# Two stacked transformer-like blocks on one core: half of the transposed activations made on VectorE

## The reference

```
h = rmsnorm(x, g_ffn1);  x = x + 0.5 * (silu(h @ w1) * (h @ w3)) @ w2      # stage "ffn0", hidden width 2816
h = rmsnorm(x, g_mix);   x = x + mixer(h @ w_in) @ w_o                     # stage "mix"
h = rmsnorm(x, g_ffn2);  x = x + 0.5 * (silu(h @ w1) * (h @ w3)) @ w2      # stage "ffn1"
```

## Time and profile before

| | |
|---|---|
| time, median of 3 runs | 2257.19 us (2256.69 to 2257.74) |
| span of the profiled execution | 2255.2 us (its time outside the span is not recorded) |
| TensorE matmuls, busy | 2249.8 us, 100%, 11686 instructions |
| TensorE weight loads, busy | 1920.7 us, 85% |
| VectorE, busy | 1546.0 us, 69%, 2179 instructions |
| ScalarE, busy | 1238.9 us, 55%, 1489 instructions |
| DMA | 417.61 MB, mean 185 GB/s |
| TensorE clock granted | full speed in every slice |

### The profile page before, as it was taken

The page is one execution under the profiler, slowest core; times in us unless marked ns, Lnnn a source line. Parts: engine busy times, 40 slices in busy tenths (PEclk is TensorE's granted clock), DMA queues, the critical chain, the costliest instruction groups (busy, mean ns, idle before and its releaser), DMA issues.

```text
span 2255.2 us, 28960 instructions
## 1 busy us (share of the span) xinstructions
PE 2249.8 (100%) x11686; PEld 1920.7 (85%) x11686; DVE 1546.0 (69%) x2179; ACT 1238.9 (55%) x1489; POOL 0.2 (0%) x4
## 2 busy tenths in 40 slices
PE   9999999999999999999999999999999999999999
PEld 8888888888888888888888888888888888888887
DVE  7764567765774566775776599767657747976773
ACT  7644445554653544654554576465555537755652
POOL 0000000000000000000000000000000000000000
PEclk9999999999999999999999999999999999999999
DMA  7556455555555455554555553545555555345553
GB/s 264 205 198 219 168 191 175 196 196 174 191 187 205 168 175 199 187 197 169 201 190 202 192 169 129 206 155 191 206 177 187 185 180 195 109 172 196 184 191 126
DMA packets 176213, 417.61 MB, mean 185 GB/s; under 512 B 16816, under 2 KB 20784, under 8 KB 176080
## 3 DMA queue, kind: packets, MB, share of 16 engines
q1 hardware_dynamic: 175936, 415.76, 53.3%
q10 hardware_dynamic: 144, 0.00, 0.0%
HBM read 414.66 MB, written 1.05 MB: 184 GB/s over the span
## 4 chain that ended last, share of the span: by engine, by line
PE 98%; DMA 1%; DVE 0%; SPq 0%; ACT 0%; issue 0%; DVEq 0%
PE psum L666 25%; PE psum L602 17%; PE psum L604 17%; PE psum L603 17%; PE psum L667 13%; PE psum L677 3%; PE psum L634 2%; PE psum L685 2%; PE psum L976 1%; DMA xt_in<-t_xt_dram 0%; PE psum L797 0%; DMA raw<-t_gate_up_1a_dram 0%; PE psum L954 0%; PE psum L817 0%; PE psum L944 0%; PE psum L966 0%
## 5 line engine op out<-in xcount | busy, mean ns | idle before, releaser
L1646 DVE TENSOR_TENSOR split_w<-raw,split_w 128x2048 fp32r<-128x2048 f32 (+1 forms) x405 | 881.1, 2182 | 285.8 <-ACT split_w L1176 284.9
L1176 ACT ACTIVATE split_w<-raw 128x2048 fp32r<-128x2048 f32 (+1 forms) x405 | 736.2, 1828 | 311.1 <-PE psum L604 288.2
L666 PE MATMUL psum<-xt,split_w 128*128 128x512 f32 x2464 | 859.2, 393 | 0.1
L667 PE MATMUL psum<-xt,split_w 128*128 128x256 f32 x2464 | 689.2, 280 | 0.0
L666 PEld LDWEIGHTS psum<-xt,split_w 128*128 128x128 f32 x2464 | 461.2, 187 | 104.3 <-DVE split_w L1646 1.3
L667 PEld LDWEIGHTS psum<-xt,split_w 128*128 128x128 f32 x2464 | 465.3, 189 | 0.3
L602 PE MATMUL psum<-split_w,xt 128*128 128x512 f32 (+1 forms) x736 | 289.5, 393 | 0.0
L604 PE MATMUL psum<-split_w,xt 128*128 128x512 f32 (+1 forms) x736 | 283.7, 385 | 0.0
L603 PE MATMUL psum<-split_w,xt 128*128 128x512 f32 (+1 forms) x736 | 283.6, 385 | 0.0
L602 PE MATMUL psum<-split_w,ht_hi 128*128 128x512 f32 x700 | 272.9, 390 | 0.0
L604 PE MATMUL psum<-split_w,ht_lo 128*128 128x512 f32 x700 | 272.5, 389 | 0.0
(11 more groups left out here) (278 smaller groups left out, 1951.2 us busy)
## 6 DMA issues: line engine op xcount, KB each, us to landing
raw<-w_in_dram SPq DMA_DIRECT2D x180, 512.0 KB, 4.4
raw<-t_gate_up_1b_dram SPq DMA_DIRECT2D x88, 512.0 KB, 4.1
raw<-t_gate_up_2a_dram SPq DMA_DIRECT2D x88, 512.0 KB, 4.1
raw<-t_gate_up_2b_dram SPq DMA_DIRECT2D x88, 512.0 KB, 4.1
raw<-t_gate_up_1a_dram SPq DMA_DIRECT2D x84, 512.0 KB, 4.1
raw<-ffn_w_down_dram SPq DMA_DIRECT2D x80, 512.0 KB, 4.2
raw<-w_a_dram SPq DMA_DIRECT2D x40, 512.0 KB, 4.4
raw<-w_b_dram SPq DMA_DIRECT2D x40, 512.0 KB, 4.4
```

The costliest lines, as they stand in the source:

```text
L666: nc.tensor.matmul(bank, whi[:, slot, w], xt[:, c, :, :], start=c == 0, stop=False)
L667: last = nc.tensor.matmul(bank[:, 0:T], wlo[:, slot, w], xt_hi[:, c, :], start=False, stop=c == DC - 1)
L1176: nc.scalar.activation(whi[:, u % HL, 0:n], raw[:, r, 0:n], ACT.Copy).then_inc(hi_done, 1)
L1646: nc.vector.tensor_tensor(wlo[:, u % HL, 0:n], raw[:, r, 0:n], whi[:, u % HL, 0:n], ALU.subtract).then_inc(w_ready, 1)
```

## The change

Half 0 of `x` at a stage change is turned by VectorE, into a new SBUF tensor, and ScalarE and VectorE read that tensor in place of PSUM. VectorE's transpose turns blocks of 32x32 inside a group of 32 partitions; here its input lies in one partition quarter and its output in another, so 16 instructions (4 quarters of the tokens by 4 quarters of the features) turn the whole half. Each handles 32 partitions by 256 elements. Half 1 stays on TensorE.

```diff
@@ buffers, behind the other tensors of the ffn stage
+        xturned = sb(ffn, "xturned", [P, DC // 2, T])
@@ tensor: x_transposes(stage) keeps half 1 alone; the three calls for half 0 go
                 blocks(u, 0, 1, HT, (0, 1), True, False, False)
-                if next_stage != "end":
-                    eng.wait_ge(done, e.after(done, ("x", next_stage, 0)))
-                    x_transposes(next_stage, 0)
                 blocks(u, 2, 1, HT, (2, 3), False, False, True)
@@ tensor, mix1 and mix2
-                wide(u, 1, MERGED, 0, 2)
-                eng.wait_ge(done, e.after(done, ("x", "ffn1", 0)))
-                x_transposes("ffn1", 0)
-                wide(u, 1, MERGED, 2, 4)
+                wide(u, 1, MERGED)
@@ scalar: def x_hi(stage, half)
+                if half == 0:
+                    eng.wait_ge(done, e.after(done, ("turned", stage)))
+                    for c in range(4):
+                        last = nc.scalar.activation(xt_hi[:, c, :], xturned[:, c, :], ACT.Copy,
+                                                    scale=vecs[:, gain + c:gain + c + 1])
+                    last.then_inc(acted, e.mark(acted, ("xt", stage, 0)))
+                    return
@@ vector: def x_lo(stage, half)
+                if half == 0:
+                    eng.wait_ge(acted, e.after(acted, ("xt", stage, 0)))
+                    for c in range(4):
+                        last = nc.vector.scalar_tensor_tensor(
+                            out=xt_lo[:, c, :], in0=xturned[:, c, :], scalar=vecs[:, gain + c:gain + c + 1],
+                            in1=xt_hi[:, c, :].bitcast(F32), op0=ALU.mult, op1=ALU.subtract)
+                        if c % 2:
+                            last.then_inc(done, e.mark(done, ("xt", stage, 0, c // 2)))
+                    return
@@ vector: new function
+            def x_turned(stage):
+
+                eng.wait_ge(done, e.after(done, ("x", stage, 0)))
+                for q in range(4):
+                    for r in range(4):
+                        src = x[32 * q:32 * q + 32, :, 0:512].rearrange("p m (c f) -> p m c f", c=4)
+                        dst = xturned[32 * r:32 * r + 32, :, :].rearrange("p c (m t) -> p m c t", m=MT)
+                        last = nc.vector.transpose(dst[:, :, :, 32 * q:32 * q + 32], src[:, :, :, 32 * r:32 * r + 32])
+                last.then_inc(done, e.mark(done, ("turned", stage)))
@@ vector, ffn_vector at s = 27 (split of unit 30 comes right behind)
                             add_to_x(2, 0, hidden=True).then_inc(done, e.mark(done, ("x", next_stage, 0)))
+                            x_turned(next_stage)
@@ vector, mix1 and mix2
                 add_to_x(0, 0).then_inc(done, e.mark(done, ("x", "ffn1", 0)))
+                x_turned("ffn1")
                 x_lo("ffn1", 0)
                 split(u0 + 33)
```

More of the change, by code:

```diff
@@ L639, in chunk, with x_transposes @@
                 return lambda m: src[:, m, c * P:(c + 1) * P]
-            def x_transposes(stage, half):
+            def x_transposes(stage):
                 for j in range(2):
-                    c = 4 * half + 2 * j
+                    c = 4 + 2 * j
                     turn(psum[:, 6 + j, :], (chunk(x, c), chunk(x, c + 1))).then_inc(
-                        small, e.mark(small, ("xt", stage, half, j)))
+                        small, e.mark(small, ("xt", stage, 1, j)))
             def mix_first(u0):
@@ L652, in mix_first @@
                 eng.wait_ge(done, e.after(done, ("x", "mix", 1)))
-                x_transposes("mix", 1)
+                x_transposes("mix")
                 wide(u0, 0, XT, 1, 2)
@@ L729, in first_two @@
                         eng.wait_ge(done, e.after(done, ("x", stage, 1)))
-                    x_transposes(stage, 1)
+                    x_transposes(stage)
                     for b in range(2):
```

## The result

The changed kernel takes 2279.04 us (2277.28 to 2279.67, 4 runs) against 2257.28; the ratio is 1.0095 (1.0082 to 1.0108): **slower by 21.8 us**. The profiled execution has a span of 2277.1 us, 21.9 more than before. A second set of runs (experiment 8) gave 1.0096 (1.0081 to 1.0111).

What follows compares the result with a forecast made beforehand. TensorE was taken to bound the kernel (98% of the chain). Ffn ends -1.5, change of block +2.9 and mixers +12.3 gave +13.7 us on the 2255.2 span, 2268.9; with 2.0 for the median 2270.9 us, range 2257 to 2285.

Steps and rivals of the forecast that it cites:

- T: Total time of the 16 VectorE transposes at a stage change, forecast 7.3 us, without overlap and 0.03 between.
- What TensorE gains: TensorE loses 8 transposes at each of 11 changes: 9.7 us, the most the change can gain.
- a set: The 8 TensorE transposes of one half at one stage change, costed at 0.88 us.
- The second rival: VectorE transposes overlap at one element a cycle, T = 5.5: sum +1.0, 2258.2 us; no change, chance 0.13.
- Ends of ffn stages: Six plain ends: TensorE stalls 0.63 us for unit 30's split against 0.88 saved, -0.25 each, -1.5 for six.
- Ends of mixers: Four ends: TensorE waits for unit 33's split, idle 4 us in each; +3.1 each, +12.3 for four.
- The change of block: From block 1 to 2, once: the split of unit 31 comes late and TensorE waits; net +2.9 us.
- The fourth rival: Clock falls to 1.2 GHz behind each 4 us stall: sum +35, 2293 us; chance 0.09 shared with longer transposes.

Runs made afterwards that it cites:

- experiment 8: The changed kernel, unaltered, run again beside the kernel before: 2278.56 us, ratio 1.0096.
- experiment 5: Kernel before, with VectorE turning half 0 only at the seven ffn ends, splits put ahead of the transposes and x_hi: 2250.52 us, ratio 0.9971.
- experiment 4: Changed kernel with each transpose writing the quarter it reads, so xturned is arranged wrongly: 2262.05 us, ratio 1.0019.
- experiment 3: Changed kernel plus 15 matmuls that nothing reads on TensorE at each of the four mixer ends: 2268.2 us, ratio 1.0048.
- experiments 1 to 9: All the follow-up runs, on edits of the changed kernel or the kernel before; their traces' wait at the start was 0.3 to 2.2 us.

## Why the prediction came out as it did

The sign, the places and the waits were right and the time lay in the range; the size was not: +13.7 forecast, +21.8 measured. That it lay in the range is in part luck. The range reached up to 2285 for transposes longer than forecast, T up to 8.5; T was 7.2, and what took the time to 2279 was the clock, which the range left to a rival.

- **What TensorE gains.** 88 transposes go, and a set is worth 0.88 us: experiment 5 shows -0.88 seven times.
- **T.** Forecast 7.3, measured 7.2, from 0.436 and not 0.425 a piece and a spacing of 0.45. That they would not overlap, read from two gaps in the earlier trace rows, decided whether there is a loss worth speaking of: experiment 4 has T = 5.7 and is 3.9 us slower than before, not 21.8. The second rival, overlapped transposes and no change, was refuted for this kernel and nearly met by experiment 4.
- **Ends of ffn stages.** -0.25 forecast, -0.46 measured: T 0.1 shorter and a restart 0.1 quicker than my sum.
- **Ends of mixers.** +3.1 forecast, +2.9 measured with the clock full (experiment 3). The chain was read rightly: `x_hi`, ScalarE's split, VectorE's split. From `x_hi`'s start to VectorE's split it took 3.54 us (362.19 to 365.73) and not 3.41, since ScalarE's reads of `xturned` were slower, 1.71 for 1.57, where I had priced the reads from SBUF at nothing.
- **The change of block.** +2.9 forecast; by waits 0.4 + 3.0 - 0.88 = +2.5, and the rest of the measured 3.9, 1.4, I put down to the clock; no filler was tried here.
- **The step that was mis-sized: the clock.** The fourth rival had it at +22 over the forecast and shared 0.09 of the chance. It happened at all five of the forecast's stalls that came to 2.8 us and more. Its size was 6.9 us at the mixers and 1.4 at the change of block, 8.3 in all, since a fall cost 1.4 to 2.3 us and not a unit's doubled time, 5.4. It belonged into the forecast's own sum: a stall of 4 us in an engine that had never stalled was the forecast's main term, and I priced its length only.
- **The start**, +2.8 in the profiled run, 1.1 of it again the clock, was in no step; the traces of experiments 1 to 9 speak for chance.

The forecast's terms as measured: -2.7 + 2.5 + 11.5 = +11.3; with 8.3 for the clock 19.6; the start and the small steps, 2.8 - 0.5, are the rest.

## What to carry to other kernels

An engine with 30% of idle time can take over work and still stop the bound one: look at what is queued behind the new work and when it is wanted, and put that first. The same 16 transposes were worth +4.1 or -0.88 us at the change of block by their order alone. When a change makes TensorE wait, ask for the wait's length and for the clock behind it, and measure the two apart with filler matmuls.

## What the runs showed of the hardware

Stalls of TensorE and the granted clock behind them: at 3.7 us the clock fell to half in all twelve cases of three traces; at 2.8 in all five; at 2.2 to 2.4 in three of six (two of the four in experiment 4, and at the start in the changed kernel's trace but not in experiment 3's); at 1.8 or less in none. Full clock came back some 3 to 6 us after TensorE went on. The fall can also come behind the stall: in the last mixer of the changed kernel TensorE went on at 2088.55 us and was granted 1.00 from 2088.5 to 2090.0, then 0.52 from 2090.0 to 2093.5. The Trainium skill (TensorE: Matmul & The Clock Gate, "HAM oscillation") describes this loss behind waits for DMA; here a wait for VectorE brings it.

A VectorE transpose of 32x256 in float32 took 0.436 us and started 0.45 after the one before where each wrote another quarter than the last; where the quarters stayed it started 0.33 to 0.37 after it and took 0.404 on average. ScalarE's four reads of `xturned` took 1.71 us from SBUF, where the four from PSUM took 1.57.
